# One 512-column product for high and low tokens in the DeltaNet input projections, with the halves added at eviction

## The reference, cut to what matters

```
proj = h @ w_in + b_in                       # h: 256 x 2048
aq, ak, av, dq, dk_, dv_, dz, ... = split_cols(proj, IN_SPLITS)
o_att = sliding_window_sink_attention(aq, ak, av, att_sinks)
qkv = silu(causal_depthwise_conv(concat([dq, dk_, dv_]), dn_conv_w))     # 4 taps over time
q, k = l2_normalize(...); v = ...
o_dn = gated_delta_rule_chunked(q, k, v, g, beta)      # per head, with a triangular solve
o_dn = gated_rms_norm(o_dn, dz, dn_norm_g)
merged = sigmoid(ga) * (o_att @ w_br_att) + sigmoid(gb) * (o_dn @ w_br_dn)
h = layer_norm(ALPHA * h + merged @ w_out)
```

## Time and profile before

| | us |
|---|---|
| median of 3 runs | 1945.42 |
| lowest, highest | 1945.41, 1946.96 |
| profiled execution | 1945.95 |
| its span | 1944.0 |
| TensorE busy in the span | 1912.1 |
| VectorE busy | 1272.8 |
| ScalarE busy | 1026.6 |

### The profile page before, as it was taken

One profiled execution on the slowest core, in us unless ns is written; L12 is line 12 of the kernel. 1 busy time (PEld: TensorE's weight loads), 2 busy tenths in 40 slices (PEclk: granted clock), 3 DMA queues, 4 the chain that ended last, 5 costly groups with the idle time before them and its releaser, 6 DMA issues.

```text
span 1944.0 us, 29842 instructions
## 1 busy us (share of the span) xinstructions
PE 1912.1 (98%) x10549; PEld 1662.1 (86%) x10549; DVE 1272.8 (65%) x2348; ACT 1026.6 (53%) x2068; POOL 37.5 (2%) x79
## 2 busy tenths in 40 slices
PE   8999999999999999999999999999999999999997
PEld 7889999999999888888888788888888888888886
DVE  6657888888888756565666697555555555555555
ACT  4446666666656545455444564545444444444442
POOL 1000000000000000000000000000000000000000
PEclk9999999999999999999999999999999999999999
DMA  8665555455445557566566455655555565655552
GB/s 312 194 161 195 116 144 118 136 135 135 112 144 122 183 163 248 195 200 200 191 213 224 153 195 196 200 187 194 193 183 186 193 194 177 230 197 195 195 195 87
DMA packets 203604, 349.65 MB, mean 180 GB/s; under 512 B 6704, under 2 KB 72448, under 8 KB 202512
## 3 DMA queue, kind: packets, MB, share of 16 engines
q1 hardware_dynamic: 200272, 334.26, 52.2%
q0 software_dynamic: 3264, 14.47, 5.2%
HBM read 344.32 MB, written 2.10 MB: 178 GB/s over the span
## 4 chain that ended last, share of the span: by engine, by line
PE 89%; DVE 5%; ACT 3%; issue 3%; DMA 0%; DVEq 0%; ACTq 0%; SPq 0%
PE dense L573 23%; PE dense L574 23%; PE dense L575 23%; PE dense L561 4%; PE dense L562 4%; PE dense L563 4%; PE chain L717 1%; DVE lo L1374 1%; ACT hi L1029 1%; PE chain L799 1%; ACT sE L1207 1%; PE chain L984 0%; PE chain L726 0%; DMA raw<-in_w_in_dram 0%; PE chain L817 0%
## 5 line engine op out<-in xcount | busy, mean ns | idle before, releaser
L1374 DVE TENSOR_TENSOR lo<-raw,hi 128x512 fp32r<-128x512 f32 x1256 | 852.8, 691 | 519.8 <-ACT hi L1029 517.3
L1029 ACT ACTIVATE hi<-raw 128x512 fp32r<-128x512 f32 x1256 | 777.4, 630 | 634.6 <-PE dense L575 604.9
L573 PE MATMUL dense<-hi,xh 128*128 128x512 f32 x1376 | 539.8, 392 | 1.5 <-DVE xl L1918 1.1
L575 PE MATMUL dense<-lo,xh 128*128 128x512 f32 x1376 | 536.0, 390 | 0.0
L574 PE MATMUL dense<-hi,xl 128*128 128x512 f32 x1376 | 535.7, 389 | 0.0
L573 PEld LDWEIGHTS dense<-hi,xh 128*128 128x128 f32 x1376 | 258.7, 188 | 55.2 <-DVE xl L1918 2.0
L575 PEld LDWEIGHTS dense<-lo,xh 128*128 128x128 f32 x1376 | 258.4, 188 | 54.4
L574 PEld LDWEIGHTS dense<-hi,xl 128*128 128x128 f32 x1376 | 258.6, 188 | 52.2
L561 PE MATMUL dense<-xh,hi 128*128 128x256 f32 x1024 | 303.2, 296 | 0.0
L563 PE MATMUL dense<-xh,lo 128*128 128x256 f32 x1024 | 289.4, 283 | 0.0
L562 PE MATMUL dense<-xl,hi 128*128 128x256 f32 x1024 | 289.2, 282 | 0.0
(11 more groups left out here) (309 smaller groups left out, 1516.4 us busy)
## 6 DMA issues: line engine op xcount, KB each, us to landing
raw<-in_w_in_dram SPq DMA_DIRECT2D x116, 1024.0 KB, 5.1
raw<-in_w_ffn_gate_dram SPq DMA_DIRECT2D x44, 1024.0 KB, 5.0
raw<-in_w_ffn_up_dram SPq DMA_DIRECT2D x44, 1024.0 KB, 5.1
raw<-in_w_ffn_down_dram SPq DMA_DIRECT2D x44, 1024.0 KB, 5.0
raw<-in_w_br_att_dram SPq DMA_DIRECT2D x16, 1024.0 KB, 5.0
raw<-in_w_br_dn_dram SPq DMA_DIRECT2D x16, 1024.0 KB, 5.0
raw<-in_w_out_dram SPq DMA_DIRECT2D x16, 1024.0 KB, 4.9
raw<-in_w_ple_gate_dram SPq DMA_DIRECT2D x16, 1024.0 KB, 5.0
```

Source lines behind the costliest of these rows:

```text
L573: pe.matmul(o, ah, hi[:, s, :], start=(k == 0), stop=False)
L575: mm = pe.matmul(o, ah, lo[:, s, :], start=False, stop=(k == nk - 1))
L1029: act.activation(hi[:, pos.slot(n), :], raw[:, slot, off:off + 512], ACT.Copy).then_inc(sem("hi_ready"), 1)
L1374: dve.tensor_tensor(lo[:, pos.slot(n), :], raw[:, slot, off:off + 512], hi[:, pos.slot(n), :].bitcast(F32), ALU.subtract).then_inc(sem("lo ...
```

## The change

`xh` and `xl` become two halves of one tile `xx` (for each 128 rows the 256 high tokens, then the 256 low ones). In `cols_quarter` the high weights are multiplied with all 512 columns at once, so that high x high arrives in columns 0 to 255 of the bank and high x low in columns 256 to 511; low x high is added to columns 0 to 255. Three products of 256 columns become one of 512 and one of 256. ScalarE evicts the second half of the bank with the bias, and VectorE then adds the first half, straight from PSUM, in one instruction of 128x512 for both banks. The semaphores `pad0` to `pad2` and `z_in` are now raised by this addition, and a new one, `low_out`, by ScalarE. `pad_in` and the z eviction keep their places on ScalarE; the additions stand at k = 9, 17 and 25 in `conv` and at k = 0 in `chain_k` on VectorE. The three transfers of norm rows and PLE bias now share one semaphore, and so do the two of the last norm.

```diff
-        xh = place("xh", [P, KT, T], F32R)
-        xl = place("xl", [P, KT, T], F32R)
+        xx = place("xx", [P, KT, 2, T], F32R)
+        xh, xl = xx[:, :, 0, :], xx[:, :, 1, :]
...
-                        o = dense[:, bank + f, 0:T]
-                        pe.matmul(o, wh, mh[:, k, :], start=(k == 0), stop=False)
-                        pe.matmul(o, wh, ml[:, k, :], start=False, stop=False)
-                        mm = pe.matmul(o, wl, mh[:, k, :], start=False, stop=(k == KT - 1))
+                        o = dense[:, bank + f, :]
+                        if k < KT - 1:
+                            pe.matmul(o, wh, flat(xx[:, k]), start=(k == 0), stop=False)
+                            mm = pe.matmul(o[:, 0:T], wl, xh[:, k, :], start=False, stop=False)
+                        else:
+                            pe.matmul(o[:, 0:T], wl, xh[:, k, :], start=False, stop=False)
+                            mm = pe.matmul(o, wh, flat(xx[:, k]), start=False, stop=True)
...
-                    r = act.activation(pad[:, f, 3:T + 3], dense[:, 2 * ((s + 1) % 2) + f, 0:T], ACT.Identity,
+                    r = act.activation(pad[:, f, 3:T + 3], dense[:, 2 * ((s + 1) % 2) + f, T:2 * T], ACT.Identity,
                                        bias=bcol[:, ds(16 * s + f + 2 * i, 1)])
-                r.then_inc(sem(f"pad{s}"), 1)
+                r.then_inc(sem("low_out"), 1)
...
-                        r = act.activation(zb[:, f, :], dense[:, f, 0:T], ACT.Identity,
+                        r = act.activation(zb[:, f, :], dense[:, f, T:2 * T], ACT.Identity,
                                            bias=bcol[:, ds(48 + f + 2 * p, 1)])
-                    r.then_inc(sem("z_in"), 1)
+                    r.then_inc(sem("low_out"), 1)
...
                 if n % 8 == 0:
+                    b0 = 2 * ((s + 1) % 2)
+                    dve.wait_ge(sem("low_out"), 4 * i + s + 1)
+                    dve.tensor_tensor(pad[:, :, 3:T + 3], dense[:, b0:b0 + 2, 0:T], pad[:, :, 3:T + 3],
+                                      ALU.add).then_inc(sem(f"pad{s}"), 1)
                     dve.wait_ge(sem(f"pad{s}"), i + 1)
...
                 if k == 0:
+                    dve.wait_ge(sem("low_out"), 4 * p + 4)
+                    dve.tensor_tensor(zb[:], dense[:, 0:2, 0:T], zb[:], ALU.add).then_inc(sem("z_in"), 1)
...
-            dve.wait_ge(sem("pb_in"), 16)
+            dve.wait_ge(sem("ln1_in"), 48)
```

More of the change, by code:

```diff
@@ L352, in flat2, with two @@
             return m.rearrange("p a b -> p (a b)")
+        def two(m):
+            return m.rearrange("p (a t) -> p a t", a=2)
         def att_cols(b):
@@ L541, in _, with cols_quarter @@
             pool.dma_start(lnb[:], A["ln_mix_b"][0].partition_broadcast(P)).then_inc(sem("ln1_in"), 16)
-            pool.dma_start(pb[:], A["b_ple_gate"][0].partition_broadcast(P)).then_inc(sem("pb_in"), 16)
+            pool.dma_start(pb[:], A["b_ple_gate"][0].partition_broadcast(P)).then_inc(sem("ln1_in"), 16)
             pool.wait_ge(sem("quarter_done"), 4 * U_DOWN)
-            pool.dma_start(lng2[:], A["ln_ffn_g"][0].partition_broadcast(P)).then_inc(sem("ln2_in"), 16)
-            pool.dma_start(lnb2[:], A["ln_ffn_b"][0].partition_broadcast(P)).then_inc(sem("ln2_in"), 16)
+            pool.dma_start(lng2[:], A["ln_ffn_g"][0].partition_broadcast(P)).then_inc(sem("ln1_in"), 16)
+            pool.dma_start(lnb2[:], A["ln_ffn_b"][0].partition_broadcast(P)).then_inc(sem("ln1_in"), 16)
         @block.tensor
         def _(pe):
-            def cols_quarter(pos, n, j, bank, mh, ml):
+            def cols_quarter(pos, n, j, bank):
                 pe.wait_ge(sem("lo_ready"), pos.val(n + 1))
@@ L873, in mixer_turn @@
                             pe.wait_ge(sem("pad1"), i + 1)
-                    cols_quarter(pos, k, k % 8, 2 * ((s + 1) % 2), xh, xl)
+                    cols_quarter(pos, k, k % 8, 2 * ((s + 1) % 2))
                     if chain:
@@ L1035, in x_hi @@
                 act.wait_ge(sem("x_cols"), b + 1)
-                act.activation(flat(xh[:, 2 * b:2 * b + 2, :]), C[:, b % 4, :], ACT.Copy).then_inc(sem("x_hi"), 1)
+                act.activation(xh[:, 2 * b:2 * b + 2, :], two(C[:, b % 4, :]), ACT.Copy).then_inc(sem("x_hi"), 1)
             for b in range(4):
@@ L1255, in merged_hi @@
                 act.wait_ge(sem("m_cols"), b + 1)
-                act.activation(flat(xh[:, 2 * b:2 * b + 2, :]), C[:, b % 4, :], ACT.Copy,
+                act.activation(xh[:, 2 * b:2 * b + 2, :], two(C[:, b % 4, :]), ACT.Copy,
                                scale=0.5).then_inc(sem("m_hi"), 1)
@@ L1390, in x_lo @@
                 dve.wait_ge(sem("x_hi"), b + 1)
-                dve.tensor_tensor(flat(xl[:, 2 * b:2 * b + 2, :]), C[:, b % 4, :],
-                                  flat(xh[:, 2 * b:2 * b + 2, :]).bitcast(F32), ALU.subtract).then_inc(sem("x_lo"), 1)
+                dve.tensor_tensor(xl[:, 2 * b:2 * b + 2, :], two(C[:, b % 4, :]),
+                                  xh[:, 2 * b:2 * b + 2, :].bitcast(F32), ALU.subtract).then_inc(sem("x_lo"), 1)
             for b in range(4):
@@ L1813, in merged_lo @@
                 dve.wait_ge(sem("m_hi"), b + 1)
-                dve.scalar_tensor_tensor(flat(xl[:, 2 * b:2 * b + 2, :]), C[:, b % 4, :], 0.5,
-                                         flat(xh[:, 2 * b:2 * b + 2, :]).bitcast(F32), ALU.mult,
+                dve.scalar_tensor_tensor(xl[:, 2 * b:2 * b + 2, :], two(C[:, b % 4, :]), 0.5,
+                                         xh[:, 2 * b:2 * b + 2, :].bitcast(F32), ALU.mult,
                                          ALU.subtract).then_inc(sem("m_lo"), 1)
@@ L1917, in h1_lo @@
                 dve.wait_ge(sem("h1_whole"), b + 1)
-                dve.tensor_tensor(flat(xl[:, 2 * b:2 * b + 2, :]), flat(whole[:, b % 2]), flat(xh[:, 2 * b:2 * b + 2, :]).bitcast(F32),
+                dve.tensor_tensor(xl[:, 2 * b:2 * b + 2, :], whole[:, b % 2], xh[:, 2 * b:2 * b + 2, :].bitcast(F32),
                                   ALU.subtract).then_inc(sem("h1_lo"), 1)
@@ L1926, in h1_rows @@
                     dve.wait_ge(sem("h1_cols"), 2 * c + 2)
-                    dve.wait_ge(sem("ln1_in"), 32)
+                    dve.wait_ge(sem("ln1_in"), 48)
                 else:
@@ L2018, in _ @@
                 if t == 0:
-                    dve.wait_ge(sem("ln2_in"), 32)
+                    dve.wait_ge(sem("ln1_in"), 80)
                 norm([(t, slice(1024 * h, 1024 * h + 1024)) for h in range(2)], "out_rows", lng2, lnb2, lnst)
```

## The result

| | before | after |
|---|---|---|
| median, us (6 executions each, in the same rounds) | 1945.35 | 1957.40 |
| lowest, highest | 1944.97, 1946.96 | 1956.69, 1960.50 |
| profiled execution, its span | 1945.95, 1944.0 | 1958.47, 1956.5 |
| mean granted clock of TensorE in it | 0.998 | 0.995 |

The ratio is 1.0064, with an interval of 1.0053 to 1.0074: slower by 12 us. The forecast was 1951.7, with a range of 1939 to 1959. The sign and the range hold. The forecast difference, 6.3 us, is about half of the 12 that came.

A forecast was written before the change was run, and what follows sets the result against it. TensorE is busiest but already waits for VectorE, whose gapless stretch sets the pace where additions land. First stretch -1.8, six turns +8.5 and last quarters -0.4 give +6.3 on 1945.95; median forecast 1951.7 us, range 1939 to 1959.

The forecast's parts named there:

- its own case: Whole kernel: additions delay VectorE's path and the turn ends at +1.42; 1951.7 us, likeliest case alone 1948 to 1956, chance 0.48.
- heavier rival: VectorE's addition at k = 9 isn't absorbed and adds to k = 17; turn ends at 2.4, total 1958 to 1960 us, chance 0.12.
- up to the first chain product (34 quarters): First turn and into the second: no chain, TensorE sets the pace, the 34 quarters save 1.81 us.
- six turns: Loop, from k = 24 of the second turn: six turns k = 24 to k = 24, each +1.42, together +8.5 us.
- Addition at k = 25, +0.8: VectorE behind L1678, in the stretch without gaps: the addition delays all that follows, `Em` included, by 0.8 us.
- k = 0, +1.38 in all: VectorE's z addition holds up ScalarE's tanh; SiLU of z and the path to the first inverse level come 1.38 us later.
- k = 9 is absorbed: VectorE ahead of L1589: another 0.8 us, taken out by its waits of 0.51 at k = 11 and 0.49 at k = 15.
- the additions never come back: Delay at k = 9 adds to k = 17: 1958 to 1960 us, chance 0.12; sign: no VectorE idle before L1589 of step 11.
- k = 17, the wait for `Tm` from 0.82 to 1.4: TensorE's wait for L1611 grows 0.58 us, as eviction, addition and tap delay `Tm`; step 17 goes from +1.16 to +1.74.
- TensorE saves 0.0133 us in a group: Each product group takes 0.3467 us instead of 0.36; saves 0.053 a quarter, 1.7 a turn, 13.7 in the loop.
- no less than 0.32: Lower bound in us for a 512 plus 256 column pair if the longer stream hid the shorter product's weight load entirely.
- first rival: TensorE's pace decides: 1931.7 us, chance 0.09; second form, additions hide and waits stay, 1941.3, chance 0.16, if first L717 doesn't wait.

## Why the prediction was right, and where it wasn't

The mechanism holds: the change moves work from an engine that waits to the one it waits for, and the turn grows at VectorE's additions while TensorE's saving comes through only in part: a turn is 67.76 us where the additions alone made it 68.09, 0.33 less, and the 32 quarters save 32 x 0.025 = 0.8. The number is another matter. 1957.40 lies above the 1948 to 1956 that the prediction gave its own case; it is in the range only because that reached up for a heavier rival whose mechanism did not occur. In that the range held by luck. Without its three falls of the clock the profiled execution would have taken about 1953.8, inside. By terms, from the profiled executions:

| | forecast | measured |
|---|---|---|
| up to the first chain product (34 quarters) | -1.8 | -0.7 |
| the first turn with a chain, without its clock fall | -0.4 | -0.15 |
| six turns | 6 x 1.42 = 8.5 | 6 x 1.60 = 9.6 |
| three clock falls | 0 | 3 x 1.55 = 4.7 |
| sum | +6.3 | +13.4 |

The spans differ by 12.5. The 0.9 that is left lies ahead of the loop: it starts at 132.64 us before and at 131.82 after, and most of that is TensorE's first wait for the transfer of the input `x`, 7.6 and 6.9 us, which the change doesn't touch.

- *Addition at k = 25, +0.8*: right, 0.84.
- *k = 0, +1.38 in all*: right, 1.43 at L1644, 1.28 at the first inverse level.
- *k = 9 is absorbed*: right. Counted from step 24, VectorE is 2.03 us late at the first tap of k = 9 (409.74 - 376.95 against 402.84 - 372.08), 1.43 at the transpose of step 11 and 1.05 at the `lo` of step 15 (420.47), where it had waited 0.51 and 0.49 us. Leaving the addition out gains 0.04 us a turn. The rival "the additions never come back" needed 0.8 there. It named about the right total, 1958 to 1960, by a mechanism that isn't there. Its sign was badly chosen: the transpose of step 11 has no idle time before it (413.54), as the rival asked, because a delay that is absorbed uses the wait up as well.
- *k = 17, the wait for `Tm` from 0.82 to 1.4*: 1.56, more than forecast. I let `Tm` follow the tap by 0.28 us; it follows by 0.39, and by 0.38 before (421.88 to 422.26). The row for it was among those I showed, and it speaks against my reading that ScalarE's copy, not VectorE's queue, held `Tm` before. Against that, all else came to this place at +1.03 to +1.05 us in place of +1.16. The two errors cancel in the place of L733, +1.77 where I had +1.74, and add up in the wait.
- *TensorE saves 0.0133 us in a group*: mis-sized, and the first term that failed. The three products before are 0.36 from start to start. A pair of after is, by the median over the loop, 0.235 behind a 512-column product (960 distances) and 0.117 behind a 256-column one (803), 0.352: 0.008 saved, not 0.0133. Four quarters in a row take 5.74 us where they took 5.84, 0.025 a quarter where I had 0.053. One quarter of after, from its first product:

```profile
363.59 0.50 PE L566 MATMUL dense<-xx,hi 128*128 128x512 f32 x1
363.93 0.28 PE L567 MATMUL dense<-xx,lo 128*128 128x256 f32 x1
364.05 0.40 PE L566 MATMUL dense<-xx,hi 128*128 128x512 f32 x1
364.29 0.28 PE L567 MATMUL dense<-xx,lo 128*128 128x256 f32 x1
364.41 0.40 PE L566 MATMUL dense<-xx,hi 128*128 128x512 f32 x1
364.64 0.28 PE L567 MATMUL dense<-xx,lo 128*128 128x256 f32 x1
364.76 0.40 PE L566 MATMUL dense<-xx,hi 128*128 128x512 f32 x1
```

  I took each product's pace from a stage where its own size follows itself. In alternation the longer one costs 8 ns more than there and the shorter one 3 less. The bound "no less than 0.32" did not come into play at all. This term accounts for most of what is missing up to the first chain product (-0.7 for -1.8) and in the last leg of a turn (-0.20 for -0.32).
- *The clock*: not in the forecast in any form. I read that the granted clock was at its full level in the whole loop before, and did not ask what longer waits would do to it. 4.7 of the 7.1 us by which the sum is off are this.

The first rival said that the waits stay and 4.1 us come off: TensorE's first inverse level started with 1.5 us of idle time in front of it, so it fell by its own test.

What stays open: which turns have the lower clock. What the traces show is that no fall came in the loop in any kernel whose waits of TensorE for VectorE were at most 0.9 us (six kernels; none of their executions has a mean clock below 0.997); that each of the 18 falls in the six kernels that had any began 0.6 to 1.9 us behind the start of a product for which TensorE had idled 1.6 us; and that such waits don't always bring a fall: the kernel without the addition at k = 17 had none in its profiled execution, in which six turns have one of 1.49 to 1.71 us, though by the mean clock it had some in others. In the profiled executions the number of falls went up, not down, when the `Ym` wait was made shorter beside the long one for `Tm`. I found no row that tells a turn with a fall from one without before it happens, and made no run for it alone.

## What to carry to other kernels

Before giving an engine work, look whether the busiest engine already waits for it, and price the work at those places; a saving on the engine that waits is worth only what its waits let through (here 5.1 us of the 256 x 0.025 = 6.4 that the quarters save, and 3.4 with the additions in, 1960.83 - 1957.40). Then look for the order in which the added instruction stands behind what is waited for: a few reordered instructions turned +12 us into -12, of which 7.5 would have come without the change. And where a periodic wait grows, here from 0.8 to 1.6 us, look at the granted clock, of several executions: in this case shorter turns came with more falls and no shorter run.

## What was not expected of the hardware

- TensorE was busy 95% of a turn, and its clock still went to half for 3.4 us after a wait of 1.6 us, at 1.4 to 1.55 us lost each time. It came in turns spaced irregularly (the first, second and fifth of seven), though all turns have the same work, and not equally often in each execution of a kernel.
- A product of 512 columns in fp32r followed by one of 256, each with its own weights, is 0.235 + 0.117 us, where the sizes by themselves go at 0.227 and 0.12.
- The first product of a quarter behind the short chain products is slow: the quarter shown above begins at 363.59 and its second product stands at 363.93, 0.34 us on in place of 0.235. Before it was 0.20 in place of 0.12, so about 0.08 to 0.1 is lost at each such change with either size. It was in neither term of my sum, and since both kernels have it, it doesn't change their difference.
- An addition of 128x512 with one operand in PSUM lasted 0.68 to 0.69, as long as a subtraction of this size that reads SBUF alone (`lo`, 0.68 to 0.69).
